# Folding each head's sub-keys into its query weights in the expert stage of a one-layer streaming encoder

## What is computed

```python
def peer_ffn(x, w_pq, sub_keys, u_emb, v_emb):      # x: normed rows
    ...
    keys = sub_keys.astype(jnp.float32)             # (2, 8 heads, 128 keys, 128)
    def block(xb):                                  # 128 rows of 1024
        t = xb.shape[0]
        q = (xb @ w_pq).astype(jnp.float32).reshape(t, PEER_HEADS, 2, PEER_HALF)
        s = jnp.einsum('thpd,phkd->thpk', q, keys)
        top_s, top_i = lax.top_k(s, PEER_TOPK)
        ...
        best_s, best_j = lax.top_k(cand_s, PEER_TOPK)
        expert = jnp.take_along_axis(cand_i, best_j, axis=-1)
        g = jax.nn.softmax(best_s, axis=-1)
        h = jnp.einsum('td,thkd->thk', xb, u_emb[expert])
        act = (g * jax.nn.gelu(h.astype(jnp.float32), approximate=False)).astype(xb.dtype)
        return jnp.einsum('thk,thkd->td', act, v_emb[expert])
```

## Time and profile before

| What | us |
|---|---|
| Three runs, median | 3469.67 |
| Three runs, lowest and highest | 3468.79, 3473.62 |
| Span of the profiled execution | 3471.7 |
| PE, DVE, POOL, ACT busy | 2483.2, 2488.9, 1454.8, 996.6 |
| Expert stage, first DMA issue to the end of the span | 632.77 to 3471.7 |
| First gather issued | 658.93 |
| 1088 gathers, 1.05 MB each | 1140.92 MB |

### The profile page before, as it was taken

How to read it: one execution, slowest core, us unless ns; L and a number is a source line. 1 busy time by engine, 2 the same in 40 slices (tenths; PEclk the granted TensorE clock), 3 DMA queues, 4 the chain that set the end, 5 groups by cost and what they waited for, 6 DMA issues and landing times. The chain is left out here.

```text
span 3471.7 us, 41167 instructions
## 1 busy us (share of the span) xinstructions
PE 2483.2 (72%) x13379; PEld 1018.3 (29%) x13379; DVE 2488.9 (72%) x6867; ACT 996.6 (29%) x2816; POOL 1454.8 (42%) x1266
## 2 busy tenths in 40 slices
PE   7999889676667666766766676667666766766764
PEld 4444666422222222222222222222222222222221
DVE  4888678677677767776776777777777766767885
ACT  3333444322232222222222222222222222222331
POOL 2333231144444444444444444444444444535443
PEclk9999889798888888888888888878888888888877
DMA  4000200799999999999999999999999999999997
GB/s 154 27 24 21 75 31 19 276 421 421 420 412 419 420 413 418 415 416 417 416 415 416 411 412 418 419 413 416 417 419 414 413 419 416 402 366 421 413 421 328
DMA packets 194557, 1198.43 MB, mean 345 GB/s; under 512 B 31051, under 2 KB 41379, under 8 KB 55102
## 3 DMA queue, kind: packets, MB, share of 16 engines
q0 software_dynamic: 156672, 1140.92, 79.8%
q1 hardware_dynamic: 37694, 55.13, 4.6%
HBM read 1181.14 MB, written 14.84 MB: 344 GB/s over the span
## 5 line engine op out<-in xcount | busy, mean ns | idle before, releaser
L1311 PE MATMUL ps<-uv_rows,diag 64*64 64x512 f32 x8704 | 1355.1, 748 | 898.7 <-ACT diag L1433 896.9
L1220 POOL DMA_INDIRECT uv_rows<-in_uv_emb,experts x1088 | 1287.0, 1183 | 1510.2 <-PE ps L1311 1304.2
L1582 DVE CUSTOM_DVE_ANT_0 uv_rows<-uv_rows,xn_c 128x1024 f32<-128x1024 f32 x1088 | 1332.7, 1225 | 740.1 <-DMA uv_rows<-in_uv_emb,experts 734.7
L1311 PEld LDWEIGHTS ps<-uv_rows,diag 64*64 64x64 f32 x8704 | 325.4, 154 | 1638.8 <-ACT diag L1433 1206.7
L1425 ACT ACTIVATE gelu_c<-dots 128x2 f32<-128x2 f32 x544 | 110.7, 204 | 1754.1 <-DVE dots L1582 1753.9
L1433 ACT ACTIVATE diag<-ident_twice,act_c 128x64 f32<-128x64 f32 x1088 | 319.2, 340 | 286.6 <-DVE act_c L1599 285.9
L1274 PE MATMUL ps<-w_pq_sb,xnT_c 128*128 128x256 f32 x1152 | 350.5, 435 | 1.2 <-ACT xnT_c L1395 1.2
L1274 PEld LDWEIGHTS ps<-w_pq_sb,xnT_c 128*128 128x128 f32 x1152 | 223.0, 211 | 270.5 <-issue 246.8
L577 DVE SCALAR_TENSOR_TENSOR convT<-w_out_sb,tapsT,convT 128x128 f32 (+1 forms) x960 | 252.8, 343 | 0.0
L517 PE MATMUL ps<-w_in_sb,w_out_sb 128*128 128x512 f32 (+1 forms) x656 | 241.7, 524 | 12.2 <-ACT w_out_sb L403 12.2
L339 POOL TENSOR_TENSOR rstd_a<-ms_a,neg_half 128x1 f32<-128x1 f32 x9 | 85.6, 9509 | 181.1 <-ACT ms_a L384 181.1
(11 more groups left out here) (208 smaller groups left out, 2100.9 us busy)
## 6 DMA issues: line engine op xcount, KB each, us to landing
uv_rows<-in_uv_emb,experts POOLq DMA_INDIRECT x1088, 12.6
w_in_sb<-in_w_in SPq DMA_DIRECT2D x4, 2048.0 KB, 11.7
w_pq_sb<-in_w_pq SPq DMA_DIRECT2D x8, 1024.0 KB, 12.0
cat_turned<-catT SPq DMA_DIRECT2D x9, 512.0 KB, 2.6
w_out_sb<-in_x_prompt SPq DMA_DIRECT2D x8, 512.0 KB, 3.6
w_out_sb<-in_w_out SPq DMA_DIRECT2D x1, 4096.0 KB, 16.0
catT_c<-cat_turned SPq DMA_DIRECT2D x8, 512.0 KB, 8.0
out<-x_c SPq DMA_DIRECT2D x8, 512.0 KB, 8.2
```

Of the source, the lines that this page charges most:

```text
L1220: nc.gpsimd.indirect_dma_start(out=rows[:, m % RING, :], out_offset=None, in_=d.uv_emb[0], in_offset=bass.IndirectOffsetOnAxis(ap=experts[ ...
L1311: ins = pe.matmul(ps[dst, 2 * x + half, :], diag[src, (m + i) % DIAGS, :], rows[src, (m + i) % RING, cols], start=first, stop=last)
L1582: nc.vector.tensor_tensor_reduce(out=row, in0=row, in1=xn[:, block_of(n) % 2, :], scale=1.0, scalar=0.0, op0=ALU.mult, op1=ALU.add, accum_ ...
```

## The change

Since the scores are linear in the normed rows, a head's 1024 x 256 query weights can be multiplied by its two sets of 128 sub-keys once: (x W) K' = x (W K'). `fold(h)` makes this product for head h, 16 matmuls of 128 x 128 in four PSUM banks, and `fold_copied(h)` copies the four banks into `w_score`, which takes the place of `w_pq_sb` and has its size. A head's scores are then one product of 8 matmuls, `score`, whose result ACT copies straight to `half_scores`. The turn of the query, its two copies and the two score matmuls go, for every head, and so do the turns of the sub-keys.

The host now hands over the query weights of each head transposed (`w_pqT`, 128 partitions with rows of 8 KB) and the sub-keys transposed (`sub_keysT`, the same). The weights of head h are loaded into ring slot h and the sub-keys into `x1_c`. So gather m of the first eight waits for fold m, and the residual rows that belong in `x1_c` are loaded after all folds. The core of the diff:

```diff
-        w_pq = sb("w_pq_sb", [P, s.DCH, PH * PAIR])
-        keysT = sb("sub_keysT", [P, 2, PH, s.NKEYS])
+        w_score = sb("w_score", [P, PH, s.DCH, PAIR])
...
-        keys = rows[:, RING - 1, :].rearrange("p (x e) -> p x e", e=s.HALF)
-        q = sb("q_c", [P, PAIR])
-        qT = sb("qT_c", [P, 2, P])
+        keysT = x1[:, :, :].rearrange("p a n -> p (a n)").rearrange("p (h a k) -> p h a k", h=PH, a=2)
...
-            load_queries(0)
-            for p in range(2):
-                sp.dma_start(keys[:, p * PH:(p + 1) * PH, :], d.sub_keys[0, p].rearrange("h k e -> k h e")).then_inc(keys_here, 16)
-            for h in range(1, PH):
-                load_queries(h)
+            for h in range(PH):
+                sp.dma_start(rows[:, h, :], d.w_pqT[0, h]).then_inc(w_here[h], 16)
+                if h == 0:
+                    sp.dma_start(keysT[:, :, :, :], d.sub_keysT[0]).then_inc(keys_here, 16)
             cat_stored(sp)
             load_cat(1)
+            sp.wait_ge(fold_psum, FOLDS * PH)
             sp.dma_start(x1[:, 0, :], d.x1[:, :]).then_inc(x1_here, 16)
...
-                elif m == RING - 1:
-                    pool.wait_ge(keys_psum, 2)
+                else:
+                    pool.wait_ge(fold_psum, FOLDS * (m + 1))
...
+            def fold(h):
+                pe.wait_ge(w_here[h], 16)
+                if h == 0:
+                    pe.wait_ge(keys_here, 16)
+                for j in range(FOLDS):
+                    if h > 0:
+                        pe.wait_ge(fold_out, FOLDS * (h - 1) + j + 1)
+                    for i in range(2):
+                        for p in range(2):
+                            x = 2 * j + i
+                            ins = pe.matmul(ps[:, j, i * PAIR + p * s.NKEYS:i * PAIR + (p + 1) * s.NKEYS],
+                                            rows[:, h, p * s.D + x * P:p * s.D + (x + 1) * P], keysT[:, h, p, :], start=True, stop=True)
+                    ins.then_inc(fold_psum, 1)
...
+            def score(r, lo=0, hi=s.DCH):
                 b, h = route(r)
                 if lo == 0:
                     pe.wait_ge(xnT_ready, b + 1)
                     if b == 0:
-                        pe.wait_ge(w_here[h], 16)
+                        pe.wait_ge(fold_out, FOLDS * (h + 1))
                     if r > 0:
-                        pe.wait_ge(qT_out, r)
+                        pe.wait_ge(s_out, r)
                 for x in range(lo, hi):
-                    ins = pe.matmul(ps[:, Q_, 0:PAIR], xnT[:, x, :], w_pq[:, x, h * PAIR:(h + 1) * PAIR],
+                    ins = pe.matmul(ps[:, S_, 0:PAIR], xnT[:, x, :], w_score[:, h, x, :],
                                     start=(x == 0), stop=(x == s.DCH - 1))
...
+            fold(0)
             turn_rows(0)
-            query(0)
...
+            score(0)
+            fold(1)
+            score(1)
+            fold(2)
+            fold(3)
+            score(2)
+            for h in range(FIRST_ROUTED, PH):
+                fold(h)
+            score(3)
...
+            def fold_copied(h):
+                for j in range(FOLDS):
+                    act.wait_ge(fold_psum, FOLDS * h + j + 1)
+                    nc.scalar.copy(w_score[:, h, 2 * j:2 * j + 2, :],
+                                   ps[:, j, :].rearrange("p (c n) -> p c n", n=PAIR)).then_inc(fold_out, 1)
...
+            for h in range(FIRST_ROUTED, PH):
+                fold_copied(h)
+            gate_exps(0)
+            scores_out(3)
             gate_exps(1)
```

More of the change, by code:

```diff
@@ L1269, in query @@
                     if b == 0:
-                        pe.wait_ge(w_here[h], 16)
+                        pe.wait_ge(fold_out, FOLDS * (h + 1))
                     if r > 0:
-                        pe.wait_ge(qT_out, r)
+                        pe.wait_ge(s_out, r)
                 for x in range(lo, hi):
-                    ins = pe.matmul(ps[:, Q_, 0:PAIR], xnT[:, x, :], w_pq[:, x, h * PAIR:(h + 1) * PAIR],
+                    ins = pe.matmul(ps[:, S_, 0:PAIR], xnT[:, x, :], w_score[:, h, x, :],
                                     start=(x == 0), stop=(x == s.DCH - 1))
                 if hi == s.DCH:
[L1277 to L1286, removed]
-                pe.wait_ge(qT_out, r + 1)
-                if r > 0:
-                    pe.wait_ge(s_out, r)
-                for p in range(2):
-                    ins = pe.matmul(ps[:, S_, p * P:(p + 1) * P], qT[:, p, :], keysT[:, p, h, :], start=True, stop=True)
-                ins.then_inc(s_psum, 1)
+                    ins.then_inc(s_psum, 1)
             def weigh(n, k):
@@ L1336, in gains @@
                 ins.then_inc(gains_psum, 1)
-            def turn_keys(i):
-                for p in range(2):
-                    for h in range(4 * i, 4 * i + 4):
-                        ins = pe.transpose(ps[:, 2 * p + i, (h % 4) * P:(h % 4 + 1) * P], keys[:, p * PH + h, :], g.ident[:, :])
-                ins.then_inc(keys_psum, 1)
-            turn_rows(0)
-            query(0)
-            pe.wait_ge(keys_here, 32)
-            turn_keys(0)
-            for r in range(FIRST_ROUTED):
-                turn_query(r)
-                if r == 0:
-                    pe.wait_ge(keys_ready, 1)
-                score(r)
-                query(r + 1)
-                if r == 0:
-                    turn_keys(1)
-            pe.wait_ge(keys_ready, 2)
+            fold(0)
+            turn_rows(0)
+            score(0)
[7 more added lines that the diff above has]
+            score(3)
             for n in range(HEADS):
-                routed, left = routed_in(n), left_to(n)
+                routed = routed_in(n)
                 for k in range(K):
@@ L1445, in crossed @@
                 ins.then_inc(crossed_out, 1)
-            def keys_out(i):
-                act.wait_ge(keys_psum, i + 1)
-                for p in range(2):
-                    ins = nc.scalar.copy(keysT[:, p, 4 * i:4 * i + 4, :], ps[:, 2 * p + i, :].rearrange("p (h k) -> p h k", k=s.NKEYS))
-                ins.then_inc(keys_ready, 1)
-            rows_out(0)
-            for r in range(FIRST_ROUTED):
-                query_out(r)
-                if r < 2:
-                    keys_out(r)
-                turned_out(r)
-                if r == 3:
-                    gate_exps(0)
-                scores_out(r)
+            fold_copied(0)
+            rows_out(0)
+            scores_out(0)
+            fold_copied(1)
+            scores_out(1)
+            fold_copied(2)
+            fold_copied(3)
+            scores_out(2)
+            for h in range(FIRST_ROUTED, PH):
+                fold_copied(h)
+            gate_exps(0)
+            scores_out(3)
             gate_exps(1)
@@ L1464, in _ @@
             for n in range(HEADS):
-                routed, chosen, left = routed_in(n), chosen_in(n), left_to(n)
+                routed, chosen = routed_in(n), chosen_in(n)
                 for i in range(NGROUPS):
@@ L1747 @@
     laid = dict(inputs)
+    depth, halves, ph, nkeys, half = inputs["sub_keys"].shape
+    laid["w_pqT"] = np.asarray(inputs["w_pq"]).reshape(depth, -1, ph, halves, half).transpose(0, 2, 4, 3, 1).reshape(
+        depth, ph, half, -1)
+    laid["sub_keysT"] = np.asarray(inputs["sub_keys"]).transpose(0, 4, 2, 1, 3)
     laid["uv_emb"] = np.concatenate([np.asarray(inputs["u_emb"]), np.asarray(inputs["v_emb"])], axis=-1)
```

68 lines of the change are left out of this document (15 added, 53 removed).

## The result

| What | before | after |
|---|---|---|
| Median of six runs each, us | 3469.23 | 3480.61 |
| Lowest and highest, us | 3465.13, 3474.09 | 3479.06, 3485.42 |
| Ratio to before, 95% interval | | 1.0036 [1.0026, 1.0046] |
| Span of the profiled execution, us | 3471.7 | 3483.7 |
| First gather issued, us | 658.93 | 664.35 |

The changed kernel is slower by 0.36%, 11.4 us between the medians; the forecast was 3484 with +14.1. The page of the changed kernel: its span, busy times, GB/s in 40 slices (now of 87.1 us), and the loads of the weights (count, KB each, median us to landing).

What follows compares the result with a forecast made beforehand. The prediction took the DMA engines to bound the expert stage. Removed work counted 0, and folds and the late gate delayed row 8 by 14.1 us, kept to the end: 3469.7 + 14.1 = 3483.8, 3484 us, range 3471 to 3496.

Steps and rivals of the forecast that it cites:

- The bound: Expert stage: it ends when the DMA engines have moved 1088 gathers of 1 MB, at 2.49 us each; only their idle time matters.
- The removed work at 0: Main loop: the turns, score matmuls, copies and waits removed for 72 routed heads are off the path, worth 0.
- Rival 1: Expert stage: the lighter PE pays back 8 to 20 us, giving 3464 to 3476, taken as 3472; chance 0.13.
- rival 2: Expert stage: the ring loop sets the pace, not the bytes, so the kernel gets faster, 3452 us; chance 0.06.
- A fold at 3.7 us: Opening, on PE: 32 records a fold at 0.11 us each; the first takes 6.5 us at the lower clock.
- rival 3: Folds on PE: weight loads don't overlap matmuls, 3.3 us more a fold, 26 over eight, 3510 us; chance 0.06.
- First gate: Opening, on ACT: head 0's gate waits behind all eight folds' copies, at 688.7 us against 665.55 before.
- Gather 8: Opening: the ninth gather goes out after the first weighing, at 700.7 us against 679.47 before.
- Row 8 taken up: Opening, on DVE: row 8 lands 6.9 us after gather 8's issue, the queue being empty, at 707.6 us against 693.49.
- Delay of row 8: End of the opening's sum: row 8 comes 14.1 us later than before.
- The delay to the end: Rest of the expert stage: nothing is regained, so the 14.1 us stand to the last row.
- The loads, taken at nothing: Opening: 9.4 MB in 8 KB rows take 22.7 us instead of 27.1; the 4.4 us saved can't be used by the gathers.

Runs made afterwards that it cites:

- the turns back: The changed kernel with the removed copies, turns and two matmuls per head put back, unused, in the main loop (62 of 72 routed heads): 3487.26 us, ratio 1.0041.
- the loads alone: The kernel before with only the host layout changed (8 KB weight rows, sub-keys already turned), no fold: 3465.25 us, ratio 0.9977; again 3464.97 us, 0.9983.

## Why the prediction was right

**The bound.** That the DMA engines set the end, and that only their idle time counts, was the step on which all hung. It held: the byte account gives row 16's delay in eight profiles, and the body's rate is the same with 663 and with 677 us of PE.

**The removed work at 0.** Held within the noise: the turns back cost 0.0005 of the time, 1.7 us, and from row 64 to row 896 the kernels without the turns regain at most 2.3 us on before, to the last row at most 6.1. Rival 1, the pay-back of 8 to 20 us from the whole loop, is out with that. So is rival 2, the loop that sets the pace: with PE at 663 us in 1000 the DMA engines still moved 416 GB/s, and in the second execution of the changed kernel

```profile
1000.00:2000.00 1000.00, 669.64 (x3688) 218.23 (x3680) 714.00 (x1867) 250.27 (x755) 467.60 (x397) 0.82 1.01 417
```

with the same share of 1.01.

**A fold at 3.7 us, 14.4 for four, 6.5 for the first.** Measured 3.73, 14.45 and 6.53. The first two were worked out from rows. The 6.5 was set between its bounds, 3.7 and 7.4, without a working; by the first product's 5.51 against 3.62 it would be 5.6, so that it came out this close is in part luck. The group of all folds (least, median and most ns of a record):

```profile
L1262 PEld LDWEIGHTS ps<-x_c,uv_rows x256: 190/192/333, 641.9 to 686.7; 128*128 128x128 f32 x128
L1262 PE MATMUL ps<-x_c,uv_rows x256: 272/275/553, 641.9 to 686.8; 128*128 128x128 f32 x128
```

A load's record lasts 192 ns in the median and a matmul's 275, but 128 of each pass in 14.45 us, 0.113 us a pair. So the loads do run beside the matmuls, over 256 records and not four as in the earlier trace rows, and rival 3 (3.3 us more a fold, 3510) is out. The rule that the prediction set beside it, that a load overlaps a running matmul only where its row group differs, stands in the Trainium skill in "TensorE: Matmul & The Clock Gate" under "The mechanism", the section ahead of the one that the prediction named. This trace contradicts it, since every load here uses all rows. The same page of the Trainium skill says under "Step-by-step: what each phase is for" that a load may also be pulled ahead into a background weight buffer. With that the trace agrees, though at 0.113 us a pair it shows the overlap and not the buffer.

**From row to row of the opening.**

| Step | Forecast, us | Measured, us |
|---|---|---|
| Fold 0 starts | 642.3 | 641.95 |
| First choice begins | 655.3 | 654.75 |
| First gather | 664.9 | 664.35 |
| Folds 4 to 7 end, eighth gather | 688.0 | 687.1, 687.38 |
| First gate | 688.7 | 687.63 |
| First weighing | 696.7 | 695.30 |
| Gather 8 | 700.7 | 699.20 |
| Row 8 taken up | 707.6 | 706.92 |
| Delay of row 8 | 14.1 | 13.4 |

The steps run ahead of the forecast by 0.3 to 1.5 us, each by a few tenths. The largest miss in this chain is the last step but one, and the last step makes up for it by a different mechanism than the prediction gave: row 8 didn't wait for its landing. The dot at 706.92 has no idle time for DMA before it; it follows the weights at 706.78, in DVE's own order, eight rows of 2.35 us after the first dot. Gather 8 landed 6.7 us after its issue (forecast 6.9), at 705.9, a microsecond before. That the two came out within a microsecond of each other is luck, and a faster DVE would hardly have gained anything: rows 13 and 15 wait for the DMA engines again, 2.12 and 0.32 us.

**The delay to the end.** The forecast has 14.1 us to the last row. The medians give 11.4 and 14.7, the ratios (0.0036 and 0.0034 of 3469 us) 12.5 and 11.8, so the sum was some 2 us high. Part of that is this profile against others: the second one of the changed kernel was 12.6 us late at row 8. The rest came late in the stage: between rows 928 and 960, where the sample's rows are loaded, seven of the eight profiles gain 1.8 to 4.0 us on the profile of before. The loads alone, with the whole old loop, gain there too (3.1 and 1.8), and the turns back don't (0.1 lost). So the lighter loop does not explain it by itself; it may be that the one profile of before was slow there. From row 64 to the last row the five profiles with the lighter loop gain 2.9 to 6.1 us, the loads alone 2.3 and 2.8, and the turns back lose 2.7. A pay-back of a few microseconds late in the stage is thus neither shown nor excluded.

**The loads, taken at nothing.** The prediction priced the 8 KB rows at 4.4 us and said that the gathers could not use them. In the changed kernel that is so: it moves 422 GB/s up to 656 us, and then it stands empty. Where gathers can use it, the loads alone are worth 5.7 us in bytes. The forecast's 4.4 was low by 0.5 for the rate (at 424 GB/s and not 416 the 9.4 MB take 22.2 us against 27.1); of the other 0.8 us about half is the stretch from 640 to 644 us, where before moved only 310 GB/s, 0.15 MB less than at 348. The rest isn't traced.

## What to carry to other kernels

Where the DMA engines set the end, count the bytes that they miss in the stretch that a change touches: the megabytes not moved, divided by the full rate, were here what the rows behind the hole were late, within 0.3 us. Work that is done once to save work in a loop was paid in full here, since it stands ahead of the first transfers, and earned nothing that could be told apart, since the loop's engines were not the bound. When a small instruction that others wait for (here a gate of 0.3 us) comes to stand behind a batch of copies in an engine's queue, price that wait by itself: moving it, with the first gelus and diagonals, brought back 5.8 of the 13.1 us by which row 8 was late.

## What the runs showed of the hardware that was not expected

**One execution's attention stage is 7 us longer than another's.** Two executions of the changed kernel, 400 to 500 and 500 to 600 us, the first and then the second:

```profile
400.00:500.00 100.00, 85.04 (x475) 57.91 (x475) 67.58 (x171) 42.82 (x106) 29.35 (x44) 0.85 0.07 26
500.00:600.00 100.00, 93.16 (x679) 68.78 (x676) 78.25 (x166) 48.62 (x97) 17.12 (x25) 0.93 0.06 23
```

```profile
400.00:500.00 100.00, 84.40 (x447) 56.80 (x446) 62.18 (x155) 40.26 (x101) 26.06 (x38) 0.83 0.04 17
500.00:600.00 100.00, 92.89 (x655) 68.23 (x654) 78.78 (x169) 49.05 (x97) 18.93 (x28) 0.91 0.07 27
```

At 361 us the second is 0.5 us ahead, and it enters the expert stage at 640.03 where the first does at 632.71. In between, PE's granted clock is below full in both, 0.85 and 0.93 against 0.83 and 0.91: part of the time at 1.2 GHz. Whether that is the cause isn't shown. So profiles of one kernel differ by more than half of what this change cost before the changed code begins, and only a count from the stage's entry compares them. That the spread of the other runs comes from the same place isn't shown.

**The same loads at 348 and at 424 GB/s, and the slower at the higher share.** Before, with runs of 1 KB (the weights), the DMA engines show a share of 1.10 and 348 GB/s from 648 to 652 us, and from 640 to 644, where most packets are the sub-keys' runs of 512 bytes, 1.17 and 310. With rows of 8 KB in the loads alone it is 1.01 to 1.03 and 418 to 424. A share at or above 1 is thus no proof that the engines move what they can; the length of the runs is what changed between the two.
